# Expert weights loaded as whole 2 MB matrices instead of 1 MB halves, in a two-layer trunk with 32 experts

## What is computed

```python
g_sel = argmax(h @ w_gr + b_gr)                      # one of 4 groups for each token
top_v, top_i = top_k(e_logits[rows, g_sel], 2)       # two of its 8 experts
expert_id = g_sel[:, None] * 8 + top_i
...
a = xblk @ w_gate[e]                                 # rows of expert e: (rows, 1024) @ (1024, 512)
b = xblk @ w_up[e]
y = (silu(a) * b) @ w_down[e]                        # (rows, 512) @ (512, 1024)
out = segment_sum(y * gate, token)
```

## Time and profile before

| | |
|---|---|
| median of 3 runs | 1817.61 us (1816.09 to 1818.15) |
| profiled execution | 1813.75 us, its span 1811.9 us |
| TensorE, VectorE, ScalarE busy | 90%, 83%, 57% of the span |
| bytes moved | 547.6 MB, of which 402.7 MB are 384 units of 1 MB |
| mean granted TensorE clock | 0.944 |

### The profile page before, as it was taken

The page is one execution under the profiler, slowest core; times in us unless marked ns, Lnnn a source line. Parts: engine busy times, 40 slices in busy tenths (PEclk is TensorE's granted clock), DMA queues, the critical chain, the costliest instruction groups (busy, mean ns, idle before and its releaser), DMA issues. The chain is left out here.

```text
span 1811.9 us, 20023 instructions
## 1 busy us (share of the span) xinstructions
PE 1639.3 (90%) x7847; PEld 1371.4 (76%) x7847; DVE 1510.0 (83%) x1095; ACT 1030.9 (57%) x840; POOL 437.1 (24%) x227
## 2 busy tenths in 40 slices
PE   3799999996899999999999949699999999999980
PEld 3577787785788888888888749678888888888870
DVE  5988785644699999999999758679999999999966
ACT  7221112322467777777777524357777777777742
POOL 1412130220424232322223100003432322233210
PEclk8799999997799999999999969789999999999995
DMA  9699712314699999999999954169999999999947
GB/s 340 203 314 314 266 69 81 119 46 197 218 343 376 381 385 390 385 383 387 381 388 388 387 210 173 49 234 365 381 388 387 387 383 384 384 384 387 386 183 285
DMA packets 125270, 547.62 MB, mean 302 GB/s; under 512 B 24003, under 2 KB 42975, under 8 KB 76021
## 3 DMA queue, kind: packets, MB, share of 16 engines
q1 hardware_dynamic: 91934, 497.98, 72.6%
q0 software_dynamic: 18432, 33.60, 4.9%
q10 hardware_dynamic: 14808, 14.73, 2.4%
HBM read 533.61 MB, written 46.17 MB: 320 GB/s over the span
## 5 line engine op out<-in xcount | busy, mean ns | idle before, releaser
L1310 DVE TENSOR_TENSOR unit_low<-unit,unit_high 128x2048 fp32r<-128x2048 f32 x384 | 856.0, 2283 | 15.3 <-ACT unit_high L924 15.0
L924 ACT ACTIVATE unit_high<-unit 128x2048 fp32r<-128x2048 f32 x384 | 735.4, 1915 | 42.6 <-DMA unit<-in_moe_w_up_dram 17.6
L1621 PE MATMUL ps<-unit_high,block_columns_high 128*128 128x512 f32 x1024 | 407.2, 398 | 10.4 <-DVE block_columns_low L1315 10.4
L714 POOL DMA_INDIRECT expert_rows<-y_out,assignment x64 | 214.8, 3357 | 804.3 <-DVE y_out L1340 791.9
L1623 PE MATMUL ps<-unit_high,block_columns_low 128*128 128x512 f32 x1024 | 401.2, 392 | 0.0
L1622 PE MATMUL ps<-unit_low,block_columns_high 128*128 128x512 f32 x1024 | 400.8, 391 | 0.0
L1621 PEld LDWEIGHTS ps<-unit_high,block_columns_high 128*128 128x128 f32 x1024 | 194.3, 190 | 50.2 <-DVE block_columns_low L1315 11.8
L1623 PEld LDWEIGHTS ps<-unit_high,block_columns_low 128*128 128x128 f32 x1024 | 193.5, 189 | 41.5
L1622 PEld LDWEIGHTS ps<-unit_low,block_columns_high 128*128 128x128 f32 x1024 | 193.8, 189 | 38.3
L1633 PE MATMUL ps<-unit_high,act_columns_high 128*128 128x512 f32 x512 | 206.7, 404 | 9.8 <-DVE unit_low L1310 9.8
L1635 PE MATMUL ps<-unit_high,act_columns_low 128*128 128x512 f32 x512 | 201.6, 394 | 0.0
(11 more groups left out here) (225 smaller groups left out, 1962.6 us busy)
## 6 DMA issues: line engine op xcount, KB each, us to landing
unit<-in_moe_w_gate_dram SPq DMA_DIRECT2D x128, 1024.0 KB, 7.7
unit<-in_moe_w_up_dram SPq DMA_DIRECT2D x128, 1024.0 KB, 7.3
unit<-in_moe_w_down_dram SPq DMA_DIRECT2D x128, 1024.0 KB, 8.5
cond_w<-in_w_ada_dram SPq DMA_DIRECT2D x80, 512.0 KB, 5.2
y_in<-expert_rows SPq DMA_DIRECT2D x16, 1024.0 KB, 7.3
x_rows<-in_x_dram SPq DMA_DIRECT2D x8, 1024.0 KB, 9.9
cond_w<-in_w_ada_dram SPq DMA_DIRECT2D x8, 1024.0 KB, 11.1
in_w<-in_w_in_even_dram ACTq DMA_DIRECT2D x12, 512.0 KB, 7.9
```

Of the source, the lines that this page charges most:

```text
L714: g.indirect_dma_start(out=y_dram[l], out_offset=bass.IndirectOffsetOnAxis(ap=index, axis=0), in_=src[:, :], in_offset=None, bounds_check= ...
L924: a.activation(high[k][:, :], raw[i % SLOTS][:, :], ACT.Copy).then_inc(unit_high, 1)
L1310: v.tensor_tensor(low[i % SLOTS][:, :], raw[i % SLOTS][:, :], high[k][:, :].bitcast(F32), ALU.subtract)\
L1621: mm(dst, xT_hi[:, q, :], high[k][:, cols], start=q == 0, stop=False)
```

## The change

Two neighbouring buffers become one *pair* (`pair[s]`, 16 KB per partition), and a matrix is loaded whole with one transfer. The halves stay what they were, views into the pair, and ScalarE, VectorE and TensorE still work on halves. Partition p reads the same 16 KB of the matrix as before, now in one piece. The load of a pair waits for two releases instead of one (`i - SLOTS + 2`), and both halves wait for one semaphore (`pair_loaded`).

```diff
-        raw = [at(f"unit{s}", [P, UNIT], W0 + 8 * KB * s) for s in range(SLOTS)]
+        pair = [at(f"unit_pair{s}", [P, 2 * UNIT], W0 + 16 * KB * s) for s in range(SLOTS // 2)]
+        raw = [pair[s // 2][:, s % 2 * UNIT:(s % 2 + 1) * UNIT] for s in range(SLOTS)]
...
-            def load_unit(i):
+            def load_pair(i):
                 if i >= SLOTS:
-                    sp.wait_ge(unit_done, i - SLOTS + 1)
+                    sp.wait_ge(unit_done, i - SLOTS + 2)
                 n, kind = UNITS_OF[i]
...
-                    src = moe_w_down[l, e].rearrange("(p h k) d -> h p (k d)", p=P, h=2)
+                    src = moe_w_down[l, e].rearrange("(p k) d -> p (k d)", p=P)
...
-                sp.dma_start(raw[i % SLOTS][:, :], src[h]).then_inc(unit_loaded[i % SLOTS], 16)
+                s = i // 2 % (SLOTS // 2)
+                sp.dma_start(pair[s][:, :], src).then_inc(pair_loaded[s], 16)
...
-            for i in range(SLOTS):
-                load_unit(i)
+            for i in range(0, SLOTS, 2):
+                load_pair(i)
...
-                act.wait_ge(unit_loaded[i % SLOTS], 16 * (i // SLOTS + 1))
+                act.wait_ge(pair_loaded[i // 2 % (SLOTS // 2)], 16 * (i // SLOTS + 1))
```

More of the change, by code:

```diff
@@ L131, in hybrid_trunk @@
         UNIT = 2 * D
-        raw = [at(f"unit{s}", [P, UNIT], W0 + 8 * KB * s) for s in range(SLOTS)]
-        low = [at(f"unit_low{s}", [P, UNIT], W0 + 8 * KB * s, F32R) for s in range(SLOTS)]
+        pair = [at(f"unit_pair{s}", [P, 2 * UNIT], W0 + 16 * KB * s) for s in range(SLOTS // 2)]
+        raw = [pair[s // 2][:, s % 2 * UNIT:(s % 2 + 1) * UNIT] for s in range(SLOTS)]
+        low_pair = [at(f"unit_low_pair{s}", [P, 2 * UNIT], W0 + 16 * KB * s, F32R) for s in range(SLOTS // 2)]
+        low = [low_pair[s // 2][:, s % 2 * UNIT:(s % 2 + 1) * UNIT] for s in range(SLOTS)]
         high = [at(f"unit_high{k}", [P, UNIT], SE + 8 * KB * k, F32R) for k in range(len(KINDS))]
@@ L354, in hybrid_trunk @@
         final_loaded, gain1_loaded = sem("final_loaded"), sem("gain1_loaded")
-        unit_loaded = [sem(f"unit_loaded{s}") for s in range(SLOTS)]
+        pair_loaded = [sem(f"pair_loaded{s}") for s in range(SLOTS // 2)]
         unit_high, unit_low, unit_done = sem("unit_high"), sem("unit_low"), sem("unit_done")
@@ L517, in _ @@
                 sp.dma_start(xr[:, 2 * i:2 * i + 2, :], xv[:, 2 * i:2 * i + 2, :]).then_inc(x_loaded[i], 16)
-            def load_unit(i):
+            def load_pair(i):
                 if i >= SLOTS:
-                    sp.wait_ge(unit_done, i - SLOTS + 1)
+                    sp.wait_ge(unit_done, i - SLOTS + 2)
                 n, kind = UNITS_OF[i]
-                l, e, h = n // NE, n % NE, int(kind[1])
+                l, e = n // NE, n % NE
                 if kind[0] == "D":
-                    src = moe_w_down[l, e].rearrange("(p h k) d -> h p (k d)", p=P, h=2)
+                    src = moe_w_down[l, e].rearrange("(p k) d -> p (k d)", p=P)
                 else:
-                    src = (moe_w_gate if kind[0] == "G" else moe_w_up)[l, e].rearrange("(p h k) f -> h p (k f)", p=P, h=2)
-                sp.dma_start(raw[i % SLOTS][:, :], src[h]).then_inc(unit_loaded[i % SLOTS], 16)
+                    src = (moe_w_gate if kind[0] == "G" else moe_w_up)[l, e].rearrange("(p k) f -> p (k f)", p=P)
+                s = i // 2 % (SLOTS // 2)
+                sp.dma_start(pair[s][:, :], src).then_inc(pair_loaded[s], 16)
             def load_y(l, t):
@@ L565, in _ @@
             first1 = AT[NE, "G0"]
-            for i in range(SLOTS, first1 + 4):
-                load_unit(i)
+            for i in range(SLOTS, first1 + 4, 2):
+                load_pair(i)
             sp.wait_ge(unit_done, AT[NE - 1, "U1"] + 1)
@@ L581, in _ @@
                     sp.dma_start(grow[1][:, :], mod_dram[1][G_F].partition_broadcast(P)).then_inc(gain1_loaded, 16)
-            for i in range(first1 + 4, first1 + SLOTS):
-                load_unit(i)
+            for i in range(first1 + 4, first1 + SLOTS, 2):
+                load_pair(i)
             sp.wait_ge(x_mixed1, NT)
             sp.dma_start(grow[0][:, :], final_norm_g.partition_broadcast(P)).then_inc(final_loaded, 16)
-            for i in range(first1 + SLOTS, len(UNITS_OF)):
-                load_unit(i)
+            for i in range(first1 + SLOTS, len(UNITS_OF), 2):
+                load_pair(i)
             more_weights(1)
```

## The result

The changed kernel takes 1894.82 us (median of 4 runs, 1892.91 to 1895.65) against 1817.88 for the kernel before: a ratio of 1.0423, interval 1.0405 to 1.0441. It is **4.2% slower, 77 us**, where the prediction had 1821.0 in a range up to 1850. The direction that held slightly more of the chance came true; the size did not, and the time lies outside the range. The profiled execution has a span of 1893.1 us, 81 more than the one before.

What follows compares the result with a forecast made beforehand. The prediction took TensorE to bound the kernel, at 17.76 us per block. To the 1817.6 us median it added 1.6 us for the ramps and 1.8 us for late pairs, giving 1821.0 us, range 1814 to 1850.

Steps and rivals of the forecast that it cites:

- Part 2: Landing of a 2 MB pair after its issue: 7.7 to 8.2 us in steady blocks, 7.6 in the quiet ramp.
- Part 3: Loop from G1's end to the next G1's end: landing + 9.26 us; TensorE stays the bound with landings below 8.5.
- Part 5: Steady blocks with a late pair: a few over the threshold, +1.8 us over 60 blocks, bounds 0 and 30 us.
- What bounds the kernel: Steady part of both expert stages: TensorE is the bound at 17.76 us per block, not the DMA engines.
- Part 1: Issue of a pair on SyncE: once both halves are released, even half 2.72 us later, odd half as now.
- The leads of the other pairs: Gate and down pairs in steady blocks: they have room, landing about when G1 and D1 do now; no cost.
- Part 4: Ramps, the first blocks of each layer: VectorE starts the columns later and TensorE waits, together +1.6 us.
- Part 6: The rest: SyncE issues 192 transfers fewer at 0.33 us each, but it idles, so nothing gained.
- (b): Rival, steady blocks: U pairs land above 8.5 us as a rule, plainly slower, 1849 us at 9.0; chance 0.25.
- (a): Rival, all blocks: pairs land in 6.8 to 7.5 us and stay fully hidden, 1817.6 to 1818 us; chance 0.15.
- (c): Rival: fewer, longer packets leave gathers, scatters and row loads more room, gaining over 3.6 us; chance 0.05.
- (d): Rival: the transfer is cut into the old pieces, issue and semaphore still late; same as first case, no separate chance.

Runs made afterwards that it cites:

- Run 4: Changed kernel with ScalarE copying the next block's token columns before the high part of its U0 instead of after: 1818.00 us, ratio 1.0009.
- run 11: Kernel before the change, with ScalarE's copy of the token columns moved ahead of the high part of U0: 1817.20 us, ratio 1.0000.
- Run 2: Changed kernel, each pair loaded by two 1 MB transfers issued together when both halves are free, each with its own semaphore: 1821.85 us, ratio 1.0037.
- Run 9: Changed kernel with G0's four matmuls that read the low columns put last, and TensorE's wait for those columns moved there: 1863.52 us, ratio 1.0253.
- run 5: Kernel before the change, with only the up matrices loaded whole, gate and down still in halves: 1908.70 us, ratio 1.0507.
- run 6: Kernel before the change, with only gate and down matrices loaded whole, up still in halves: 1828.05 us, ratio 1.0093.
- run 1: Changed kernel, each pair loaded by two 1 MB transfers with 8 KB rows, issued together and counted on one semaphore: 1889.26 us, ratio 1.0392.

## Why the prediction was wrong, point by point

Two terms failed, the landing of a pair (Part 2: 7.7 to 8.2 us, measured 8.9) and the leg by which the landing closes the loop (Part 3: threshold 8.5, measured 7.8). With them Part 5 came to +1.8 us, where the steady blocks lost 71.

- **What bounds the kernel** (TensorE, in both steady parts): right. Run 4 brings TensorE back to 100% with late pairs, and run 11 finds nothing to gain elsewhere.
- **Part 1**, the issue times: right. The U pair goes out when G1 is done, 5.77 us after G0's start (781.89).
- **Part 2**, the landing: wrong, the first of two faults. The prediction took 7.7 to 8.2 us and reasoned that holding back the even half costs the odd one little, "since what stood before U1 in the queue was U0 itself". Run 2 shows 9.8 where it was 7.3. An account that fits the numbers, though no run takes it apart: a load has some 2.6 us that are not its transfer (5.1 less 2.5), and U0's ran beside the work ahead of it; U0's 2.5 us of transfer were then nearly done in the 2.72 before U1's issue. Issued together, 2 MB take 7.6 from the start, and the 2.6 us that gathers and scatters add come on top: 10.2, where runs 2 and 4 have 10.0 and 10.3. Both terms were in the rows: 7.6 for two MB on a quiet queue, and 7.7 against 5.1 for one MB in the steady and the quiet part. I took the larger of the two where the sum was due. The 7.6 itself was right: the first U pair issued in each expert stage lands after 7.7 and 7.6 us.
  The estimate from the Trainium skill, page "DMA: Bandwidth & Descriptors", section "Anatomy of one DMA — SWDGE (gpsimd) path", 6.8 us, was further off. That fit is for DMAs that GpSimd issues, and SyncE issues these. The trace disagrees with it: the quickest U pair of the steady part landed after 7.5 us.
- **Part 3**, the loop: the mechanism was right, the path one leg short, the second fault. I closed it through the low part of G1 (landing + 9.26, threshold 8.5). The low columns are also read by the first matmuls of G0, which comes before: landing + 9.93, threshold 7.8. The row was among those shown, a wait of 1.91 us before G0 for the low columns, and even used for the ramp. Run 9 separates the two legs, 9.93 and 9.41: 31 us for 0.5 of threshold. With the landings of the changed kernel, a threshold of 8.5 would have given an excess of 39 us in place of 60.
- **The leads of the other pairs**: ScalarE waits for D and G pairs too (165 us), but up pairs alone give the whole loss (run 5). Gate and down alone cost 13.5 us (run 6), where Part 3 gave them nothing and my expectation at most 6.
- **Part 4**, +1.6 us in the ramps: nearly right. TensorE's waits in the first blocks grew by 1.3 us. For the low part of D0, for which it never waited there before, it now waits 0.6 us in layer 0 and 0.5 in layer 1, and for the low columns 6.2 where it was 6.0 and 4.4 as before:

```profile
PE ps L1624 <- DVE block_columns_low L1318: 6.2, 3, 2.4
PE ps L1636 <- DVE unit_low_pair L1313: 0.6, 1, 0.6
...
PE ps L1624 <- DVE block_columns_low L1318: 4.4, 2, 2.4
PE ps L1636 <- DVE unit_low_pair L1313: 0.5, 1, 0.5
```

  Two stretches at the lower clock in these blocks come on top, which Part 4 did not have.
- **Part 5**, +1.8 us of late pairs: the term that was mis-sized. About seven in ten of the steady U pairs (38 of 55) land above 7.8 us, and the mean of all 55 is 8.9. A threshold of 7.8 instead of 8.5 and a landing of 8.9 instead of 7.9 turn "few" into "most", and 1.8 us into 60. No sum of the prediction has a term for the lower clock, which took another 11 in these blocks.
- **Part 6**: right; half the issues bring nothing (run 1).
- **Rivals**: (b) is what happened. Its price of 1 us per us and block was right, but it counted from 8.5: at a mean of 8.9 it would have given 24 us. It had 0.25, and its "against" was the median of single units, which the change takes away. (a) and (c) fell, (d) did not apply.

## What to carry to other kernels

A prefetch that is loaded in larger lumps gives up lead twice: it starts when the last part of the buffer is free, and is usable when the last byte is in; and the time before and after a transfer, which separate loads hid behind each other, came back here (U1 after 10.0 us in run 2, 7.4 before). Before one makes that trade, one should find which consumer closes the loop from "buffer freed" to "next buffer freed", with *every* reader of each intermediate, and compare the landing *of the new transfer under the load of the steady part* with what the loop leaves over. Where such a loop is the cause, moving one short operation ahead of the late one (here a copy of 1.0 us) can be worth all of it, 77 us, while it is worth nothing in a kernel whose loop is open.

## What the hardware showed that I had not expected

**The clock answers to some of these waits.** One of the seven blocks that were longer than the loop, number 21: TensorE's first matmul.

```profile
870.70 0.79 PE L1624 MATMUL ps<-unit_high,block_columns_high 128*128 128x512 f32 x1 [2.34 <-DVE block_columns_low L1318]
```

The stretches around it (the number after POOL is the granted clock):

```profile
865.00:870.00 5.00, 3.36 (x17) 2.70 (x15) 1.39 (x3) 3.43 (x3) 0.00 (x0) 1.00 1.01 389
870.00:873.00 3.00, 2.30 (x6) 1.82 (x6) 3.00 (x3) 1.94 (x3) 0.00 (x0) 0.59 0.96 386
873.00:878.00 5.00, 5.00 (x21) 4.10 (x20) 5.00 (x3) 3.58 (x3) 0.00 (x0) 0.90 0.64 271
```

TensorE had waited 2.34 us. The granted clock then fell to the lower level, 1.2 GHz: the first matmul of 512 columns takes 0.79 us and the next ones 0.63 instead of 0.39. From one issue of a U pair to the next the block takes 21.87 us, 1.5 more than the loop gives (a landing of 10.43 and 9.93, 20.36). There are nine such stretches inside the expert stages of the changed kernel, none in the steady part of the kernel before: some 15 us that stand in no row of waits. Each began within 1.5 us of the end of a wait of 1.9 to 2.8 us for the low columns. But a wait does not always bring one: five more of 2.2 to 2.6 us in steady blocks had none, and what decides is not shown.

**Gathers and scatters of 64 rows weigh more than their bytes.** They move about 0.5 MB in a block beside 6.3 MB of weights, yet a 1 MB unit lands 7.7 us after its issue with them and 5.1 without. Of the difference, 1.1 us is there when the first of the 16 DMA engines reports (5.3 against 4.3 us, medians); the rest is the spread from the first to the last, 2.5 us against 0.9.
